# A causal mask added to the scores by VectorE in PSUM, and no longer by a TensorE product

## The chip, the cores and the metric

The kernel runs on one core of one Trainium2 chip. The metric is the device time of one execution in microseconds (us); a kernel's time is the median of several runs. The core's engines work side by side, each on its own queue of instructions, in the order written: TensorE (PE in the profile: PE for its matmuls, PEld for its weight loads), VectorE (DVE), ScalarE (ACT), GpSimd (POOL) and SyncE (SP), which issues DMAs. They wait for each other by semaphores. SBUF is the working memory; PSUM is the memory that TensorE writes its sums to, and VectorE and ScalarE can read and write it too.

## The reference, cut to what matters

The program is two blocks over a sequence of 1024 tokens with model width 1024. The second block has two kinds of attention, eight heads of each: softmax attention with a forgetting term ("fox"), and stick-breaking attention. Both are causal.

```python
# softmax ("fox"): keys up to and with the query's own position
logits = einsum('bhqd,bhkd->bhqk', q, k) * scale + F[..., :, None] - F[:, :, None, :]
logits = where(kpos[None, :] <= qpos[:, None], logits, -inf)
p = softmax(logits, axis=-1)

# stick-breaking: keys strictly before the query's position
mask = kpos[None, :] < qpos[:, None]
z = einsum('bhqd,bhkd->bhqk', q, k) * scale
log_beta = log_sigmoid(z)
log_one_minus = where(mask, log_sigmoid(-z), 0.0)
after = lax.cumsum(log_one_minus, axis=3, reverse=True) - log_one_minus
weights = where(mask, exp(log_beta + after), 0.0)
```

Queries are done in blocks of 128. A block needs the keys up to its own block, and only the last 128 x 128 block of its scores, the one on the diagonal, holds masked positions.

## The kernel before, in words

The change touches the attention stage of the second block, which in the trace runs from about 1230 to 1780 us. The stage has 8 rounds, taken in turn from the two kinds: rounds 0, 2, 4 and 6 are stick-breaking, 1, 3, 5 and 7 softmax. A round does two heads with 8 query tiles each, so 16 tiles; there are 128 tiles in all, numbered g. Tile tt of a head (0 to 7) has scores of 128 queries by w = (tt + 1) * 128 keys. The scores lie in a pair of PSUM banks, `Z[g % 2]`: one pair has the name S in the profile, the other G.

The stage is one software pipeline with a step s for each tile, written out by hand. Each engine walks over the same steps and does in each what is listed here, in this order.

- TensorE (PE): the scores of tile s + 2 (`scores`, lines 2079 and 2080: a product with the high part of the queries and one with the low part, for each 512 columns; line 2082: the mask). Then a piece of the projection of queries, keys and values for the next round (`piece`, line 2052). Then the product of the copied probabilities of tile s - 1 with the values (`values`, line 2110). Then the transposes of the probabilities of tile s (`turned`, line 2092). At two steps of a round also the transposes of the values (line 2120) and of the output (line 2131).
- ScalarE (ACT), stick-breaking: `not_taken` of tile s + 1 (line 2271, sigmoid of the negated scores), `probs_copied` of tile s - 1 (line 2265, out of PSUM), `taken` of tile s + 1 (line 2276, sigmoid). Between them, at given steps, it rounds queries, keys and weights to their high parts (`q_high` 2244 and 2245, `k_high` 2251, `w_high` 2236), turns out the output of the round before (2297) and sums its squares (2289).
- VectorE (DVE), stick-breaking: `chain` of tile s + 1. It is a scan over the negated sigmoids (line 2508, called "first") and a product with the sigmoids ("made", line 2511). In softmax rounds it is one custom instruction (line 2501). At given steps also `evac` (line 2471, which empties the projection's bank J to SBUF), `q_low` after tile 6 and `k_low` after tile 11 (lines 2479 and 2486, the low parts, two instructions each for the two heads), and `out_of` (2522 to 2526). The evacuation of a half of the projection comes ahead of the chain of its step.
- GpSimd (POOL): the low part of the next weights (line 1989, `w_lo`) as soon as ScalarE has made the high part, and in softmax rounds the mask (below).

Apart from the very first pieces, the projection is summed in one bank, J. So TensorE can begin a new half of it only after VectorE has evacuated the one before.

The mask is a constant of 128 x 128 bf16 values (`maskb`, one for each kind: 0 where a key is allowed, a large value elsewhere). In softmax rounds 1, 3 and 5 GpSimd adds it to the forget sums ahead of time (`mask_in_sums` is true, line 1980). In the four stick-breaking rounds and the last softmax round TensorE adds it: a product of the identity (`identb`) with the mask into the diagonal block of the scores, as the last product of the group. That is 5 rounds of 16 tiles, 80 products.

A wait such as `S.wait(act, "pe", "z", g)` holds the engine named first until the engine named second has done the step with that name and number. `do` marks such a step on VectorE and `me` is VectorE's wait for one of its own.

Of the kernel before, what the change touches and what calls it, by code (L numbers as in the profile page):

```python
# [9 lines left out]
ALU = mybir.AluOpType  # L10
# [4 lines left out]
P = 128  # L15
# [144 lines left out]
def program(nc, a, out, known):  # L160
# [27 lines left out]
    identb, maskb = bits[:, 0, :].bitcast(BF16), bits[:, 1:3, :].bitcast(BF16)  # L188
# [31 lines left out]
    S = Steps(known)  # L220
# [230 lines left out]
    with nc.Block() as block:  # L451
# [1272 lines left out]
        TILES, STEPS, SHIFT = 2 * TT, 2 * TT * 2 * HEADS, 2  # L1724
# [34 lines left out]
        Z = [S2, G[1]]  # L1759
# [5 lines left out]
        def tile_of(g):  # L1765

            return X[g // TILES % 2], g % TILES // TT, g % TT
# [11 lines left out]
        def mask_in_sums(g):  # L1779

            return tile_of(g)[0] == "f" and g // TILES < ROUNDS - 1

        def last_group(g):
            return GROUP_AT[g][-1][0] if g >= 0 else -1
# [4 lines left out]
        def stream(s):  # L1789

            q, n = divmod(s + SHIFT, TILES)
            return q + 1, n
# [36 lines left out]
        def own_rows(hh):  # L1829
            return slice(HD * hh, HD * hh + HD)  # L1830
# [176 lines left out]
        def _(pe):  # L2007
# [17 lines left out]
            for x, name in enumerate(("out sum", "out scaled sum")):  # L2025
                S.wait(pe, "dve", name, KT - 1)
                for t in range(TT):
                    mm = pe.matmul(G[1][:, x * TT + t:x * TT + t + 1], bs[:, x, t * P:(t + 1) * P], ones[:, 0:1], start=True, stop=True)
# [29 lines left out]
            def read(g):  # L2058

                S.wait(pe, *(("dve", "first", g) if tile_of(g)[0] == "f" else ("act", "taken", g)))  # L2060

            def scores(g):

                x, hh, tt = tile_of(g)
                r = g // TILES
                (Qh, Ql, Ks, _), z, w = SETS[r % 2], Z[g % 2], (tt + 1) * P
                if g < 2:
                    S.wait(pe, "act", ("rstd12 copied", "rstd1 copied")[g], 1)
                else:
                    read(g - 2)  # L2070
                if g > TILES and g % TILES == 5:
                    S.wait(pe, "act", "outT", 2 * (r - 1))
                if g % TILES == 0:
                    S.wait(pe, "act", "k high", r)
                    S.wait(pe, "dve", "k low", r)
                t = slice(tt * P, (tt + 1) * P)
                for b in range((w + NB - 1) // NB):
                    cols = slice(b * NB, min(w, (b + 1) * NB))
                    pe.matmul(z[:, cols], Qh[hh][:, t], Ks[hh][:, cols], start=True, stop=False)  # L2079
                    mm = pe.matmul(z[:, cols], Ql[hh][:, t], Ks[hh][:, cols], start=False, stop=mask_in_sums(g) or tt // 4 != b)  # L2080
                if not mask_in_sums(g):
                    mm = pe.matmul(z[:, tt * P:w], identb, maskb[:, "fs".index(x), :], start=False, stop=True)
                S.mark("pe", "z", mm, g)

            def turned(g):
# [123 lines left out]
        def _(act):  # L2209
# [56 lines left out]

            def not_taken(g):
                w = (g % TT + 1) * P
                S.wait(act, "pe", "z", g)
                S.wait(act, "dve", "first", g - 2 if g % TILES else g - 1)  # L2270
                S.mark("act", "not", act.activation(nots[g % 2][:, 0:w], Z[g % 2][:, 0:w], ACT.Sigmoid, scale=-1.0), g)

# [142 lines left out]
        def _(v):  # L2415
            def do(name, ins, turn=None):
                S.mark("dve", name, ins, turn)
                return name

            def me(name, turn=None):  # L2420
                S.wait(v, "dve", name, turn)
# [51 lines left out]
            def q_low(q):  # L2473
                Qh, Ql = SETS[q % 2][0:2]
                S.wait(v, "pe", "z", TILES * (q - 1) - 1)
                for hh in range(2):
                    S.wait(v, "act", f"q high {hh}", q)
                    own = own_rows(hh)
                    ins = v.tensor_tensor(Ql[hh][own, :], qt[own, :], Qh[hh][own, :].bitcast(F32), ALU.subtract)
                do("q low", ins, q)  # L2480

            def k_low(q):
                Ks = SETS[q % 2][2]
                S.wait(v, "act", "k high", q)
                for hh in range(2):
                    ins = v.tensor_tensor(Ks[hh][other_rows(hh), :], qt[own_rows(hh), :], Ks[hh][own_rows(hh), :].bitcast(F32), ALU.subtract)
                do("k low", ins, q)

            def chain(g):
                x, hh, tt = tile_of(g)  # L2490
                w = (tt + 1) * P
                p = pr[g % 2][:, 0:w]
                if x == "f":
                    r = g // TILES
                    if mask_in_sums(g):
                        S.wait(v, "pool", "masked", g)
                    elif tt == 0:
                        v.wait_ge(nf_landed[hh], 16 * (r // 2 + 1))
                    S.wait(v, "pe", "turned", last_group(g - 2))
                    S.wait(v, "pe", "z", g)  # L2500
                    do("first", v.tensor_tensor_reduce(out=p, in0=(masked_sums if mask_in_sums(g) else fsum[hh])[:, 0:w], in1=Z[g % 2][:, 0:w], scale=1.0, scalar=1e30,
                                                       op0=ALU.add, op1=ALU.min, accum_out=mn[:, g % 2, :]), g)
                else:
                    S.wait(v, "act", "not", g)
                    if g % TILES:
                        me("made", g - 1)
                    n_ = nots[g % 2]
                    do("first", v.tensor_tensor_scan(left[:, T - w:T][:, ::-1], n_[:, 0:w][:, ::-1], n_[:, 0:w], 1.0, ALU.mult, ALU.bypass), g)
                    S.wait(v, "act", "taken", g)
                    me("first", g)  # L2510
                    do("made", v.tensor_tensor(p, p, left[:, T - w + 1:T + 1], ALU.mult), g)

            def out_of(g4):
                x, hh, t0 = tile_of(4 * g4)
                r, n0 = 4 * g4 // TILES, 4 * g4 % TILES
                S.wait(v, "pe", "values", last_group(4 * g4 + 3))
                if g4 % 4 == 0 and r:
                    S.wait(v, "pe", "out turned", 2 * r - 1)
                    S.wait(v, "act", "square", TT * r - 1)
                dst, src = ON[:, t0:t0 + 4, own_rows(hh)], V[:, 0:4 * HD].rearrange("p (b d) -> p b d", d=HD)  # L2520
                if x == "f":
                    do("row sums", v.reciprocal(rs[:, n0:n0 + 4], rs[:, n0:n0 + 4]), g4)
                    me("row sums", g4)
                    do("out", v.tensor_tensor(dst, src, rs[:, n0:n0 + 4].unsqueeze(2).to_broadcast([P, 4, HD]), ALU.mult), g4)
                else:
                    do("out", v.tensor_copy(dst, src), g4)
# [8 lines left out]
            for s in range(-TILES - SHIFT, STEPS + 1):  # L2535
                q, n = stream(s)
                if n == 0 and 1 <= q <= ROUNDS:
                    evac(q - 1, 5)
                if q < ROUNDS and n in EVAC_AT[q % 2]:
                    evac(q, EVAC_AT[q % 2][n])  # L2540
                if s >= 5 and s % 4 == 1:
                    out_of((s - 5) // 4)
                if 0 <= s + 1 < STEPS:
                    chain(s + 1)
                if q < ROUNDS:
                    if n == 7:
                        q_low(q)
                    if n == 12:
                        k_low(q)
                if s == -TILES:  # L2550
                    S.wait(v, "act", "f ln")
                    do("forget logs", v.scalar_tensor_tensor(g8, g8, 0.0, l8, ALU.min, ALU.subtract))
                    me("forget logs")
                    do("forget sums", v.tensor_tensor_scan(F8, g8, g8, 0.0, ALU.add, ALU.bypass))
                if s == STEPS - TT:
                    v.wait_ge(x2_landed, 16 * KT)
                if s >= STEPS - TT and s % 2:
                    normed((s - STEPS + TT) // 2)
                if s == STEPS - 2:
                    S.wait(v, "act", "square", TT * (ROUNDS - 1) - 1)  # L2560
                    do("sb squares", v.tensor_reduce(ss[:, 0, :], ssp.rearrange("p (i x) t -> p x t i", x=2)[:, 0], AX.X, ALU.add))
                if s == STEPS - 1:
                    S.wait(v, "act", "sb root")
                    do("sb rstd", v.reciprocal(ss[:, 0, :], ss[:, 0, :]))
                    me("sb rstd")
                    diagonals("sb", bs[:, 0, :], ss[:, 0, :])
# [775 lines left out]
```

## Time and profile before

| | us |
|---|---|
| Median of 3 runs | 2575.83 |
| Lowest and highest | 2574.42, 2577.51 |
| The profiled execution, its own time | 2574.28 |
| Its span in the profile | 2572.5 |
| TensorE busy (matmuls) | 2506.5 |
| VectorE busy | 1509.0 |
| ScalarE busy | 1030.1 |
| GpSimd busy | 1058.9 |

The span runs from the first to the last instruction of the profile. Busy time counts a matmul from its start to its modelled end, and neighbouring matmuls overlap, so what a product costs is read from the starts of the products around it. Granted clock is the share of full speed that TensorE was given. In a timeline row the columns are start, duration, engine, line, operation, output and inputs with their shapes, and the count of instructions merged into the row (x2 means two, back to back). In square brackets stands how long the engine sat idle before it, and what ended that. The letter before the arrow is the tile that is written. Some names are shared by buffers that lie at one place: `forget_sums` in a row of line 2271 or 2508 is the second buffer of negated sigmoids, and G is the second pair of score banks, the bank J, or the bank that the values' product is summed in, by the line.

### The profile page before, as it was taken

The numbers are of one execution on the slowest core, as the hardware profiler recorded it, in microseconds if no ns is written. First come the engines' busy times: TensorE is split into PE (matmuls) and PEld (weight loads), VectorE is DVE, ScalarE is ACT, GpSimd is POOL, SyncE is SP. The second block draws the span as 40 slices with busy tenths as digits, with TensorE's granted clock in tenths as the row PEclk, the third lists the DMA queues.
The fourth block names the chain that finished last, engine by engine and source line by source line (L and its number), as shares of the span: only waits on it lengthen the run. The fifth ranks groups of instructions, "written<-read, shape, count | busy, mean of one in ns | idle before, by whom it ended". The sixth has DMA issues, their size and how long they took to land. (4 is left out here: it accounts for less than half of the span.)

```text
span 2572.5 us, 31716 instructions
## 1 busy us (share of the span) xinstructions
PE 2506.5 (97%) x12610; PEld 2089.5 (81%) x12610; DVE 1509.0 (59%) x1462; ACT 1030.1 (40%) x1528; POOL 1058.9 (41%) x617
## 2 busy tenths in 40 slices
PE   8999999999999999999999999999989999999999
PEld 4888788888888888887788888887867888888887
DVE  5864557665666753445645545464986667675324
ACT  3421043435344430024455655565344444443214
POOL 3765453333434335543111111213467777862320
PEclk9999999999999999999999999999989999999999
DMA  8222231211212144342111011013212222235311
GB/s 343 82 89 72 95 96 52 68 58 66 71 68 76 50 181 146 98 139 82 34 42 42 34 41 42 25 51 131 103 45 92 81 74 99 74 109 228 129 41 66
DMA packets 66238, 226.07 MB, mean 88 GB/s; under 512 B 7816, under 2 KB 11784, under 8 KB 64816
## 3 DMA queue, kind: packets, MB, share of 16 engines
q1 hardware_dynamic: 49824, 169.00, 18.5%
q10 hardware_dynamic: 16272, 55.09, 6.0%
q8 instruction: 99, 1.62, 0.3%
q14 instruction: 43, 0.35, 0.0%
HBM read 174.22 MB, written 45.65 MB: 85 GB/s over the span
## 5 line engine op out<-in xcount | busy, mean ns | idle before, releaser
L264 POOL TENSOR_TENSOR w_hi<-w_raw,ones 128x1024 fp32r<-128x1024 f32 x67 | 178.7, 2667 | 525.8 <-PE G L238 471.9
L269 POOL TENSOR_TENSOR w_lo<-w_raw,w_hi 128x1024 fp32r<-128x1024 f32 x88 | 239.2, 2718 | 198.0 <-ACT w_hi L263 192.8
L238 PE MATMUL G<-H_hi,w_hi 128*128 128x512 f32 x928 | 290.1, 394 | 1.0 <-ACT silu_zB L724 0.7
L238 PE MATMUL G<-H_lo,w_hi 128*128 128x512 f32 x928 | 285.9, 389 | 0.0
L238 PE MATMUL G<-H_hi,w_lo 128*128 128x512 f32 x928 | 285.8, 389 | 0.0
L238 PEld LDWEIGHTS G<-H_lo,w_hi 128*128 128x128 f32 x928 | 174.2, 188 | 36.6
L238 PEld LDWEIGHTS G<-H_hi,w_lo 128*128 128x128 f32 x928 | 174.2, 188 | 36.5
L238 PEld LDWEIGHTS G<-H_hi,w_hi 128*128 128x128 f32 x928 | 171.6, 188 | 36.9 <-issue 3.7
L1989 POOL TENSOR_TENSOR w_lo<-w_raw,w_hi 128x1024 fp32r<-128x1024 f32 x24 | 60.1, 2506 | 319.8 <-ACT w_hi L2236 319.8
L2110 PEld LDWEIGHTS G<-att_v,probsT 128*128 128x128 f32 x1152 | 147.0, 192 | 24.5 <-ACT probsT L2265 13.8
L2052 PE MATMUL G<-A_hi,w_hi 128*128 128x512 f32 x368 | 152.8, 415 | 9.4 <-DVE projected L2471 8.4
L2110 PE MATMUL G<-att_v,probsT 128*128 128x64 f32 x1152 | 145.7, 272 | 12.2 <-ACT probsT L2265 9.6
L2052 PE MATMUL G<-A_hi,w_lo 128*128 128x512 f32 x368 | 144.9, 394 | 0.0
L2052 PE MATMUL G<-A_lo,w_hi 128*128 128x512 f32 x368 | 144.5, 393 | 0.0
L2265 ACT ACTIVATE probsT<-U 128x512 f32<-128x512 f32 (+1 forms) x192 | 86.7, 486 | 128.3 <-PE U L2092 127.7
L2851 PE MATMUL G<-sums_hi,up_hi_S 128*128 128x512 f32 x260 | 102.4, 394 | 5.3 <-POOL up_lo_S L2801 4.8
L2851 PE MATMUL G<-sums_lo,up_hi_S 128*128 128x512 f32 x260 | 102.1, 393 | 0.0
L2851 PE MATMUL G<-sums_hi,up_lo_S 128*128 128x512 f32 x260 | 102.1, 393 | 0.0
L2801 POOL TENSOR_TENSOR up_lo<-up_raw,up_hi 128x512 fp32r<-128x512 f32 x66 | 88.3, 1339 | 17.7 <-ACT up_hi L1909 17.7
L1274 ACT ACTIVATE exps<-exps 128x1024 f32<-128x1024 f32 x60 | 61.9, 1057 | 71.2 <-DVE exps L1433 64.3
L2052 PEld LDWEIGHTS G<-A_hi,w_hi 128*128 128x128 f32 x368 | 70.2, 191 | 22.4 <-DVE projected L2471 7.0
L2092 PE MATMUL U<-ident,probs 128*128 128x128 f32 x576 | 85.6, 276 | 0.0
(594 smaller groups left out, 6263.4 us busy)
## 6 DMA issues: line engine op xcount, KB each, us to landing
w_raw<-w_in SPq DMA_DIRECT2D x65, 512.0 KB, 3.3
up_raw<-w_up SPq DMA_DIRECT2D x44, 512.0 KB, 5.0
pre_raw<-w_in SPq DMA_DIRECT2D x30, 512.0 KB, 3.3
act_d<-made SPq DMA_DIRECT2D x22, 512.0 KB, 2.9
wm<-w_mod SPq DMA_DIRECT2D x8, 1024.0 KB, 18.5
w_raw<-w_out SPq DMA_DIRECT2D x16, 512.0 KB, 3.3
x_d<-x ACTq DMA_DIRECT2D x16, 512.0 KB, 2.9
x<-x_d SPq DMA_DIRECT2D x16, 512.0 KB, 9.1
```

Of the source, the lines that this page charges most:

```text
L238: mm = nc.tensor.matmul(dst[:, n * NB:n * NB + c], w[:, k, :], m[:, k, n * NB:n * NB + c], start=first, stop=last)
L264: eng.tensor_tensor(dst, src, ones.unsqueeze(1).to_broadcast([P, kt, P]), ALU.mult)
L269: nc.gpsimd.tensor_tensor(w_lo[:, slot, 0:kt, :], w_raw[:, slot, 0:kt, :], w_hi[:, slot, 0:kt, :].bitcast(F32), ALU.subtract).then_inc(w_r ...
L1274: S.mark("act", f"exps {w} {e}", act.activation(E[e], src, ACT.Exp, scale=1.0 / GATE_NORM), h)
L1989: g.tensor_tensor(w_lo[:, j % 2], w_raw[:, j % 2], w_hi[:, j % 2].bitcast(F32), ALU.subtract).then_inc(w_ready, 1)
L2052: mm = pe.matmul(bank, w[:, j % 2, k, :], m[:, k, cols], start=first, stop=last)
L2092: mm = pe.transpose(bank[:, b * P:(b + 1) * P], pr[g % 2][:, (b0 + b) * P:(b0 + b + 1) * P], ident)
L2110: mm = pe.matmul(V[:, at:at + HD], pT[c % 2][:, b, :], v[:, b0 + b, own_rows(hh)], start=b0 + b == 0, stop=b0 + b == tt)
L2265: S.mark("act", "p copied", act.activation(pT[c % 2][:, 0:n, :], blocks_of(bank_of_u(("p", c)), n), ACT.Copy), c)
L2801: S.mark("pool", f"low {name}", g_.tensor_tensor(slot_lo[name], slab_source(p, name), slot_hi[name].bitcast(F32), ALU.subtract), p)
L2851: mm = pe.matmul(dst, w[name][:, j, :], up_moving(name, x, j), start=first and j == 0 and w is slot_hi and x == 0, stop=j == PAIRS_OF - 1 ...
```

## The change

The identity product goes. The last low-part product of each 512 columns now closes its group, and the scores are signalled right after it. VectorE gets a new step `z_masked(g)`: it waits for the scores of tile g and adds the mask to their diagonal block, in place in PSUM. It is called for tile g + 1 right behind the first instruction of tile g's chain, so in a stick-breaking round between the scan and the product of tile g. ScalarE's `not_taken` waits for that step and no longer for TensorE. In the last softmax round the custom instruction waits for it. Rounds 1, 3 and 5 keep the mask in the forget sums. For tile 0 the step is called ahead of the first chain.

```diff
                     pe.matmul(z[:, cols], Qh[hh][:, t], Ks[hh][:, cols], start=True, stop=False)
-                    mm = pe.matmul(z[:, cols], Ql[hh][:, t], Ks[hh][:, cols], start=False, stop=mask_in_sums(g) or tt // 4 != b)
-                if not mask_in_sums(g):
-                    mm = pe.matmul(z[:, tt * P:w], identb, maskb[:, "fs".index(x), :], start=False, stop=True)
+                    mm = pe.matmul(z[:, cols], Ql[hh][:, t], Ks[hh][:, cols], start=False, stop=True)
                 S.mark("pe", "z", mm, g)
...
             def not_taken(g):
                 w = (g % TT + 1) * P
-                S.wait(act, "pe", "z", g)
+                S.wait(act, "dve", "z masked", g)
                 S.wait(act, "dve", "first", g - 2 if g % TILES else g - 1)
...
+            def z_masked(g):
+
+                if g == STEPS or mask_in_sums(g):
+                    return
+                x, _, tt = tile_of(g)
+                block = Z[g % 2][:, tt * P:(tt + 1) * P]
+                S.wait(v, "pe", "z", g)
+                do("z masked", v.tensor_tensor(block, block, maskb[:, "fs".index(x), :], ALU.add), g)
...
                     S.wait(v, "pe", "turned", last_group(g - 2))
-                    S.wait(v, "pe", "z", g)
+                    if mask_in_sums(g):
+                        S.wait(v, "pe", "z", g)
+                    else:
+                        me("z masked", g)
                     do("first", v.tensor_tensor_reduce(...), g)
+                    z_masked(g + 1)
                 else:
                     ...
                     do("first", v.tensor_tensor_scan(left[:, T - w:T][:, ::-1], n_[:, 0:w][:, ::-1], n_[:, 0:w], 1.0, ALU.mult, ALU.bypass), g)
+                    z_masked(g + 1)
                     S.wait(v, "act", "taken", g)
                     me("first", g)
                     do("made", v.tensor_tensor(p, p, left[:, T - w + 1:T + 1], ALU.mult), g)
...
+                if s + 2 == 0:
+                    z_masked(0)
                 if 0 <= s + 1 < STEPS:
                     chain(s + 1)
```

## Rows read from the trace of the kernel before

**Rows 1.** The page, busy time of each engine, its share of the span, instructions.

```profile
PE 2506.5 (97%) x12610; PEld 2089.5 (81%) x12610; DVE 1509.0 (59%) x1462; ACT 1030.1 (40%) x1528; POOL 1058.9 (41%) x617
```

**Rows 2.** Busy time by stretches: round 4, last round; then PEclk, DMA share, GB/s.

```profile
1514.00:1584.00 70.00, 67.50 (x423) 57.90 (x422) 48.13 (x47) 42.82 (x87) 7.99 (x4) 1.00 0.11 38
1724.00:1772.00 48.00, 41.62 (x304) 37.15 (x302) 20.37 (x44) 32.09 (x80) 21.14 (x9) 0.93 0.55 209
```

**Rows 3.** Line 2082, one bank pair; timelines of TensorE, with the mask and without.

```profile
L2082 PE MATMUL S<-bf_constants x40: 229/230/303, 1230.5 to 1766.9; 128*128 128x128 bf16 x40
...
1568.64 0.28 PE L2080 MATMUL G<-k_parts,q_lo 128*128 128x256 f32 x1
...
1569.11 0.39 PE L2052 MATMUL G<-A_lo,w_hi 128*128 128x512 f32 x1
...
1302.71 0.28 PE L2080 MATMUL G<-k_parts,q_lo 128*128 128x256 f32 x1
...
1303.07 0.40 PE L2052 MATMUL G<-A_lo,w_hi 128*128 128x512 f32 x1
```

**Rows 4.** Waits from 1200 to 1790: who for whom, us, times, longest.

```profile
PE G L2052 <- DVE projected L2471: 8.4, 11, 2.8
```

**Rows 5.** Timeline of round 4, TensorE's wait for the copied probabilities of tile 2.

```profile
1535.17 0.88 PE L2110 MATMUL G<-att_v,probsT 128*128 128x64 f32 x6 [1.23 <-ACT probsT L2265]
```

**Rows 6.** Timeline of round 4, tiles 6 and 7, all engines.

```profile
1542.18 2.03 DVE L2508 TENSOR_TENSOR_SCAN left_over<-not_taken 128x896 f32<-128x896 f32 x1 [0.66 <-ACT not_taken L2271]
...
1544.19 0.39 PE L2080 MATMUL G<-k_parts,q_lo 128*128 128x512 f32 x1
1544.31 1.09 DVE L2511 TENSOR_TENSOR probs<-probs,left_over 128x896 f32<-128x896 f32 x1
...
1545.32 2.44 DVE L2479 TENSOR_TENSOR q_lo<-projected,q_hi 64x1024 fp32r<-64x1024 f32 x2
...
1546.90 3.10 POOL L1989 TENSOR_TENSOR w_lo<-w_raw,w_hi 128x1024 fp32r<-128x1024 f32 x1 [25.05 <-ACT w_hi L2236]
...
1547.85 0.69 DVE L2471 SCALAR_TENSOR_TENSOR projected<-G,rstd 128x512 f32<-128x512 f32 x1
...
1548.60 0.50 PE L2052 MATMUL G<-A_hi,w_hi 128*128 128x512 f32 x1 [0.55 <-DVE projected L2471]
```

**Rows 7.** Timeline of round 4, product of tile 11 and the low keys.

```profile
1566.24 0.69 DVE L2511 TENSOR_TENSOR probs<-probs,left_over 128x512 f32<-128x512 f32 x1
...
1566.81 2.38 POOL L1989 TENSOR_TENSOR w_lo<-w_raw,w_hi 128x1024 fp32r<-128x1024 f32 x1 [16.81 <-ACT w_hi L2236]
1566.97 4.54 DVE L2486 TENSOR_TENSOR k_parts<-projected,k_parts 64x1024 fp32r<-64x1024 f32 x2
```

**Rows 8.** Timeline of round 4, tiles 11 to 13.

```profile
1569.23 0.82 ACT L2271 ACTIVATE forget_sums<-G 128x768 f32<-128x768 f32 x1
...
1571.53 0.60 ACT L2265 ACTIVATE probsT<-U 128x512 f32<-128x512 f32 x1 [1.48 <-PE U L2092]
...
1571.60 0.69 DVE L2471 SCALAR_TENSOR_TENSOR projected<-G,rstd 128x512 f32<-128x512 f32 x1
...
1572.21 1.48 DVE L2508 TENSOR_TENSOR_SCAN left_over<-not_taken 128x640 f32<-128x640 f32 x1
...
1574.54 1.00 PE L2110 MATMUL G<-att_v,probsT 128*128 128x64 f32 x8
```

**Rows 9.** Groups by line and shape: count, busy us, mean ns, idle before.

```profile
L2511 DVE TENSOR_TENSOR probs<-probs,left_over 128x128 f32<-128x128 f32 x8 | 2.3, 292 | 2.7 <-ACT probs L2276 1.8 <-ACT forget_sums L2271 0.5
```

**Rows 10.** Timeline of round 0, tiles 6 and 7.

```profile
1260.46 1.09 DVE L2511 TENSOR_TENSOR probs<-probs,left_over 128x896 f32<-128x896 f32 x1
...
1260.99 0.39 PE L2080 MATMUL G<-k_parts,q_lo 128*128 128x512 f32 x1
...
1263.24 2.93 POOL L1989 TENSOR_TENSOR w_lo<-w_raw,w_hi 128x1024 fp32r<-128x1024 f32 x1 [22.07 <-ACT w_hi L2236]
...
1264.75 0.50 PE L2052 MATMUL G<-A_hi,w_hi 128*128 128x512 f32 x1
```

## The prediction

> **What bounds the kernel now.** I read the page first, then the busy time by stretches over the attention stage, then the line of the removed product, then the waits, and last the timeline of one stick-breaking round, instruction by instruction. TensorE is busy for 97% of the span [rows 1]. In a stick-breaking round of 70 us it is busy for 67.5 us at a granted clock of 1.00, while VectorE is busy for 48.1 us and ScalarE for 42.8 us [rows 2]. So the end is set by TensorE's stream, and a product taken from it is worth something. But the 2.5 us that TensorE does not work in such a round are a few waits at fixed places: for the probabilities that ScalarE copies back (1.23 us at 1535.17), and for VectorE to empty the one bank J in which the next round's projection is summed (0.55 us at 1548.60) [rows 5, 6]. Over the stage TensorE waits 8.4 us, 11 times, for that evacuation [rows 4]. At these places VectorE is the later one, and the change gives VectorE more to do there.
>
> I number the 16 tiles of a round 0 to 15 (widths 128 to 1024, twice). In step s TensorE does scores(s+2), a piece of projection, values(s-1), turned(s). VectorE does the scan and the product of tile s+1. ScalarE does, strictly in this order, `not` of s+1, the copy of the turned probabilities of s-1, `taken` of s+1.
>
> **What is removed.** 80 products of the identity with the mask [rows 3]; the row shows the 40 of one pair of banks, and the other pair has as many. What one costs TensorE is not its 0.23 us, since products overlap. From the start of the last low product of a 256-wide tile to the start of the second projection product behind it, it is 1569.11 - 1568.64 = 0.47 us with the mask and 1303.07 - 1302.71 = 0.36 us without [rows 3]. So 0.11 us each, 8.8 us for 80 if all were kept.
>
> Not all are kept. A saving ahead of a wait whose releaser is not TensorE itself only makes the wait longer. Going through round 4 (1514 to 1584): tiles 0 to 4 lie ahead of the turning of the previous round's output, which starts the chain of ScalarE that ends in the wait of 1535.17, so they are kept. Tiles 5 and 6 are lost in that wait and in the one for the evacuation behind it, 7 and 8 in the wait of 1548.60. Tiles 9 and 10 are kept. Tiles 11 to 14 are lost, since the evacuation at 1571.60 to 1572.29 [rows 8] releases the piece behind the scores of tile 14. Tile 15 is kept. That is 8 kept masks in rounds 2, 4 and 6 and 7 in round 0, where tile 0 stands before a wait: 31 x 0.11 = 3.4 us. In the last round (softmax, no projection) TensorE is busy for 41.6 of 48 us [rows 2], so its waits are long enough to swallow the savings. VectorE's next instruction there waits for a transpose that TensorE does after the scores anyway, so the additions hide. I put both at nothing; the bounds are 16 x 0.11 = 1.8 us gained and 16 x 0.29 = 4.6 us lost.
>
> **What is added.** 80 additions on VectorE of 128 columns. The nearest row is the 128-wide tensor_tensor of the same engine, 0.292 us [rows 9]. The bounds are nothing (it would fill the gap that the scan-to-product dependency leaves anyway, 1544.21 to 1544.31 in [rows 6]) and 0.69 us, the 512-wide evacuation out of PSUM. I take 0.29. If its scores are ready when the scan ends, the addition fills that gap, its start overlapping the scan's end by 0.09 us as neighbouring instructions of this engine do, and the product behind it is hardly moved. 14 of the 16 additions of a round are of this kind or stand where VectorE waits for ScalarE anyway, and cost nothing. Two places do not.
>
> **Place one, tile 7, the projection's bank.** The added instruction stands between scan 6 and product 6 and waits for the scores of tile 7. Behind it on VectorE stand product 6, the two halves of `q_low`, and the evacuation of J for which TensorE already waits. Scan 6 ends at 1544.21. The last low product of tile 7 ends at 1544.19 + 0.39 = 1544.58, so the addition runs from 1544.62 to 1544.91, and product 6 starts at 1544.82, not 1544.31: half a microsecond late [rows 6]. The first half of `q_low` then runs from 1545.83 to 1547.05, not 1545.32 to 1546.54.
>
> Now GpSimd comes in. Its split of the weights (`w_lo`) starts at 1546.90, released by ScalarE, which this delay does not touch. Before, it met the second half of `q_low` already running: it took 3.10 us, not 2.38 [rows 6, 7], and VectorE was not held. After, it is waiting when the first half ends, with the second not begun. What happens then is in the same trace: at 1566.81 GpSimd started 0.12 us before a VectorE product ended, and the `k_low` that came next took 4.54 us for two halves that need 2.44 as `q_low` does: it stood still for 2.10 us, until about the end of GpSimd's instruction at 1569.19 [rows 6, 7]. So the second half of `q_low` ends where GpSimd has had its turn, 1547.05 + 2.1 + 1.22 = 1550.37. The evacuation follows to 1551.15, and TensorE's piece goes at 1551.20, not 1548.60: 2.60 us lost. The addition itself has one input in PSUM, as the evacuation has, which ran its plain 0.69 us inside GpSimd's instruction.
>
> The Trainium skill ("SBUF — State Buffer", section "Who interferes with whom") says it as a rule: a VectorE instruction with two SBUF inputs and a GpSimd instruction that reads SBUF exclude each other, and the one that issues first holds the port for its whole length. These rows agree. By that rule alone the order at 1547 decides; did they share the port by halves, the place would cost about the 0.5 us of delay.
>
> In round 0 the same place has no wait yet, but the step is shorter: the scores of tile 7 end at 1260.99 + 0.39 = 1261.38, when product 6 had already been running since 1260.46. The first half of `q_low` would run 1262.63 to 1263.85, with GpSimd waiting from 1263.24 (0.6 us, no close call), the second half ends at 1267.17, the evacuation at 1267.95, and the piece of 1264.75 goes at 1268.01: 3.26 us [rows 10]. Sum of place one: 3.3 + 3 x 2.6 = 11.1 us.
>
> **Place two, tile 13, the copied probabilities.** Before, `not` 13 needed the scores alone and ran at 1569.23. Now it needs addition 13, which stands behind scan 12, and scan 12 stands behind `k_low` and an evacuation: 1572.21 to 1573.69. Addition 13 ends at 1573.89, `not` 13 takes 1573.93 to 1574.75. Behind it on ScalarE stands the copy of the turned probabilities of tile 11, which was done at 1572.13: it now takes 1574.65 to 1575.25. TensorE wanted them at 1574.54 and gets them at 1575.28 [rows 8]. 0.74 us, in each of the four rounds: 3.0 us. An addition of no length would still cost 0.45 us here.
>
> **The sum.** 11.1 + 3.0 - 3.4 = +10.7 us. The profiled execution took 2574.28 us (span 2572.5 and 1.8 around it), which gives 2585.0. It stands 1.5 us under the median of the three runs, 2575.83, so I say 2586 for a median.
>
> **Rivals.**
> *The port falls the other way (20%).* In rounds 2, 4 and 6 GpSimd is ahead of the second half of `q_low` by only 0.15 us; with an addition under 0.14 us, or scores signalled earlier, it comes too late. Against it: 0.12 us were enough at 1566.93 [rows 7]. Then place one costs 0.5 us in three rounds and 3.3 in round 0: 3.3 + 1.5 + 3.0 - 3.4 = +4.4, near 2580.
>
> *Only the gain (15%).* VectorE is idle for 22 of 70 us [rows 2] and the additions are done in these; the two places do not reach TensorE, because it comes early to them. That decides if product 6 starts no later than now and `not` 13 is not behind `k_low`. Against it: both are fixed by the order on the engines. It gives -3.4 us with the kept masks and -8.8 with all: 2572 to 2567. This is the rival on the other side.
>
> *Costs and gain even out (13%).* Place two only, with place one absorbed, is 3.0 - 3.4 = -0.4: 2575.5.
>
> *The forecast (52%)*: 2586, its own range 2583 to 2590. The upper end has an addition of 0.69 us: 0.4 us more at each of eight places, +3.2.
>
> A difference under 0.2% (5.2 us, 2570.7 to 2581.0) can't be told from none. Faster: most of the second rival, 0.14. Within: the evened case and over half of the first rival, 0.25. Slower: the forecast and the rest of the first, 0.61. The range 2571 to 2591 leaves out most of the second rival and a little above.
>
> **What would show it.** In the trace after: product 6 of an even round starts 0.5 us after scan 6 ends; the second half of `q_low` is long (x2 about 4.5 us, not 2.44); TensorE's wait for J in step 6 is near 3 us in four rounds, and TensorE's total wait for the evacuation goes from 8.4 to about 19 us; the values of tile 11 wait 0.7 us or more for the copy; GpSimd's split there takes 2.4 to 2.6 us. The softmax rounds 1, 3 and 5 keep their length. The forecast is wrong if `q_low` keeps 2.44 us, if the addition takes well under 0.2 us, or if the stick-breaking rounds are not longer than their 70 us.

## The result, and the profile after

The changed kernel takes 2594.19 us (median of 4 runs, 2593.89 to 2596.45), the kernel before on the same chip 2576.67 us (4 runs, 2574.42 to 2580.73). The ratio is 1.0064, 95% interval 1.0051 to 1.0077: about 16.5 us slower (the two medians lie 17.5 us apart). The forecast was 2586 with a range of 2571 to 2591. The direction was right; the time lies above the range.

The profiled execution of the changed kernel has a span of 2592.6 us where the one of before has 2572.5. The page's first part answers to [rows 1]. TensorE has 80 instructions less, VectorE 80 more and 17 us more of work, and TensorE's busy time has not fallen, although products were removed:

```profile
PE 2507.3 (97%) x12530; PEld 2093.3 (81%) x12530; DVE 1526.1 (59%) x1542; ACT 1030.9 (40%) x1528; POOL 1055.7 (41%) x617
```

The added instruction, by form, over the attention stage (operation and shape, count, busy us, mean ns, idle before it). It answers to [rows 9], from which it was priced at 292 ns:

```profile
L2494 DVE TENSOR_TENSOR G<-G,bf_constants 128x128 f32<-128x128 f32 x40 | 11.5, 288 | 16.2 <-PE G L2080 15.8
L2494 DVE TENSOR_TENSOR S<-S,bf_constants 128x128 f32<-128x128 f32 x40 | 11.4, 285 | 16.5 <-PE S L2080 16.1
```

The waits from 1200 to 1810 (who for whom, us, times, longest) answer to [rows 4]. TensorE's wait for the evacuated bank went from 8.4 to 22.1 us, forecast about 19. Its wait for the copied probabilities, 9.6 us in 12 waits before, is 3.2 us more in 17:

```profile
PE G L2052 <- DVE projected L2469: 22.1, 16, 3.7
PE G L2108 <- ACT probsT L2263: 12.8, 17, 2.1
```

**Place one** in the timeline of round 4 (start us, us, what, idle before) answers to [rows 6]. Round 4 began later, so only distances compare:

```profile
1552.05 2.02 DVE L2519 TENSOR_TENSOR_SCAN left_over<-not_taken 128x896 f32<-128x896 f32 x1 [0.61 <-ACT not_taken L2269]
...
1554.56 0.30 DVE L2494 TENSOR_TENSOR G<-G,bf_constants 128x128 f32<-128x128 f32 x1 [0.49 <-PE G L2080]
...
1554.77 1.08 DVE L2523 TENSOR_TENSOR probs<-probs,left_over 128x896 f32<-128x896 f32 x1
...
1555.77 4.51 DVE L2477 TENSOR_TENSOR q_lo<-projected,q_hi 64x1024 fp32r<-64x1024 f32 x2
...
1556.77 2.42 POOL L1989 TENSOR_TENSOR w_lo<-w_raw,w_hi 128x1024 fp32r<-128x1024 f32 x1 [24.67 <-ACT w_hi L2234]
...
1560.37 0.69 DVE L2469 SCALAR_TENSOR_TENSOR projected<-G,rstd 128x512 f32<-128x512 f32 x1
...
1561.12 0.80 PE L2052 MATMUL G<-A_hi,w_hi 128*128 128x512 f32 x1 [3.33 <-DVE projected L2469]
...
1561.71 0.63 PE L2052 MATMUL G<-A_lo,w_hi 128*128 128x512 f32 x1
```

Scan 6 ends at 1554.07; the addition waits for TensorE's scores and the product follows 0.70 us after the scan. GpSimd's split, pending before the second half of `q_low` can begin, goes first, and the two halves of `q_low` take 4.51 us for 2.44. All of this was forecast. The last two rows were not, though one of [rows 3] shows what belongs there: the products behind the wait take 0.63 us and start 0.43 apart, where others take 0.39 and start 0.23 apart.

One thing at this place was not read before the change: GpSimd's turn cost VectorE time there as well, only later. Scan 7, right behind the evacuation, took 3.69 us in the kernel before, where GpSimd's split lasts until 1550.00 [rows 6], and 2.28 us in the changed one, in which GpSimd has finished by then. The first row is of before, the second of after:

```profile
1548.46 3.69 DVE L2508 TENSOR_TENSOR_SCAN left_over<-forget_sums 128x1024 f32<-128x1024 f32 x1
1560.98 2.28 DVE L2519 TENSOR_TENSOR_SCAN left_over<-forget_sums 128x1024 f32<-128x1024 f32 x1
```

So VectorE stood still for 1.4 us behind the evacuation before, and stands still for 2.1 us ahead of it now. What the change moved is the place of the stop, from where TensorE does not wait to where it does.

**Place two** in the same round, which answers to [rows 8]:

```profile
1586.74 1.48 DVE L2519 TENSOR_TENSOR_SCAN left_over<-not_taken 128x640 f32<-128x640 f32 x1
...
1588.14 0.28 DVE L2494 TENSOR_TENSOR G<-G,bf_constants 128x128 f32<-128x128 f32 x1
...
1588.45 0.81 ACT L2269 ACTIVATE forget_sums<-G 128x768 f32<-128x768 f32 x1 [4.82 <-DVE G L2494]
...
1589.15 0.59 ACT L2263 ACTIVATE probsT<-U 128x512 f32<-128x512 f32 x1
...
1589.80 1.10 PE L2108 MATMUL G<-att_v,probsT 128*128 128x64 f32 x8 [0.57 <-ACT probsT L2263]
```

**The clock.** Two stretches of 4 us, behind the long wait of round 4 and of round 0. The columns are those of [rows 2]; the seventh is the granted clock. TensorE is busy for nearly all of each, and at 1.2 GHz (0.50) all through the first. In rounds 2 and 6 the clock behind the wait is 0.62 (it falls a little later there) and 0.50:

```profile
1561.00:1565.00 4.00, 3.88 (x9) 3.11 (x10) 3.90 (x5) 0.28 (x1) 0.00 (x0) 0.50 0.16 61
1269.00:1273.00 4.00, 3.85 (x11) 3.12 (x11) 3.90 (x5) 0.28 (x1) 0.00 (x0) 0.57 0.10 40
```

**Where the span went.** I measure a round from one turning of its values to the next. Stick-breaking rounds 0, 2, 4 and 6 went from 68.8, 72.1, 72.1 and 69.3 us to 75.3, 76.4, 77.1 and 74.3: +6.5, +4.3, +5.0 and +5.0. The three softmax rounds between them lost 1.1 us together (0.24, 0.27 and 0.62), and the last round 0.7. That sums to the 18.9 us by which the stage ends later (1777.43 to 1796.30); the other 1.2 us of span lie behind the stage and were not followed. The scores of tiles 0 and 1 of a round are made ahead of its turning, so they count to the round ahead: in the kernel before, the mask products of these tiles of round 4 stand at 1509.95 and 1514.46, its turning at 1516.66.

### The profile page after: what moved, and what is told of

It is laid out like the page before. It is cut to its first block and busy times, and to the rows that moved or that the text cites. A ratio compares the mean times of both kernels' runs of the same rounds, so it can differ in the third digit from the quotient of the medians.

```text
span 2592.6 us, 31636 instructions
## 1 busy us (share of the span) xinstructions
PE 2507.3 (97%) x12530; PEld 2093.3 (81%) x12530; DVE 1526.1 (59%) x1542; ACT 1030.9 (40%) x1528; POOL 1055.7 (41%) x617
## 5 line engine op out<-in xcount | busy, mean ns | idle before, releaser
L2052 PE MATMUL G<-A_hi,w_hi 128*128 128x512 f32 x368 | 151.6, 412 | 22.4 <-DVE projected L2469 22.1
```

The source lines that it names most:

```text
L2052: mm = pe.matmul(bank, w[:, j % 2, k, :], m[:, k, cols], start=first, stop=last)
```

## The experiments

Each kernel was timed side by side with the kernel before on the same chip, 5 to 11 executions each (medians of before 2578.6 for e1 to e4, 2577.6 for e5 to e8). An interval of a ratio is some 0.09 to 0.14% on either side, 2.3 to 3.6 us, so the ratios tell the large steps apart, and the smaller ones are read from the lengths of rounds in the profiles, one execution for each kernel. The order here is that of the argument.

**e1: the gain by itself.** The kernel before without the 80 products and with nothing in their place.

```
-  mm = pe.matmul(z[:, cols], Ql[hh][:, t], Ks[hh][:, cols], start=False, stop=mask_in_sums(g) or tt // 4 != b)
-  if not mask_in_sums(g):
-      mm = pe.matmul(z[:, tt * P:w], identb, maskb[:, "fs".index(x), :], start=False, stop=True)
+  mm = pe.matmul(z[:, cols], Ql[hh][:, t], Ks[hh][:, cols], start=False, stop=True)
```

> The kernel before with the 80 mask products left out and nothing in their place, so the mask of the stick-breaking rounds and of the last softmax round is not applied. It gives the gain alone. My step of the prediction (31 masks kept at 0.11 us): 3.4 us faster, near 2573. Rival, every mask is kept: 8.8 us faster, near 2568. Rival, all is absorbed by waits: no difference.

Measured: 2574.63 us, ratio 0.9983 (0.9974 to 0.9992), so 4.4 us. The stage took 3.4 us less from its first turning to its end than before. So the waits swallow about half of the 8.8 us or more, as forecast; both rivals, 8.8 and nothing, lie outside the interval. By rounds it is less tidy: rounds 2, 4 and 6 lost 0.8 us each, the softmax rounds 0.2 to 0.3 each, the last round 0.9, and round 0 grew by 0.5.

**e2: place one by itself.** The kernel before, with its products, and the addition of tile 7 alone, four in all. The mask is added there a second time.

```
+  if g % TILES == 6:
+      z_masked(g + 1)          # between scan 6 and product 6
   S.wait(v, "act", "taken", g)
...
-  S.wait(act, "pe", "z", g)    # in not_taken
+  S.wait(act, *(("dve", "z masked", g) if g % TILES == 7 else ("pe", "z", g)))
```

> The kernel before, product kept, with one VectorE addition in each stick-breaking round: that of tile 7, between scan and product of tile 6 (it adds the mask a second time). 4 additions of 80. If place one (the wait for the scores of tile 7, then GpSimd taking the port ahead of the second half of q_low, then a clock at half) is nearly all of the loss: +18 to +21 us, near 2596, with waits of 2.8 to 3.7 us for the bank and a granted clock of 0.5 for some 5 us behind each. Rival, the loss comes from 80 additions spread over the stage: under +2 us.

Measured: 2595.86 us (2594.61 to 2597.52), ratio 1.0068 (1.0054 to 1.0081). Four additions of the 80 cost as much as the whole change, products kept. Its timeline in round 4 has the same chain:

```profile
1556.98 4.52 DVE L2479 TENSOR_TENSOR q_lo<-projected,q_hi 64x1024 fp32r<-64x1024 f32 x2
...
1557.96 2.46 POOL L1989 TENSOR_TENSOR w_lo<-w_raw,w_hi 128x1024 fp32r<-128x1024 f32 x1 [25.04 <-ACT w_hi L2236]
...
1562.33 0.50 PE L2052 MATMUL G<-A_hi,w_hi 128*128 128x512 f32 x1 [3.19 <-DVE projected L2471]
...
1564.63 0.63 PE L2052 MATMUL G<-A_hi,w_lo 128*128 128x512 f32 x1
```

The wait is 3.19 us, and here too the products behind it grow to 0.63 us, after some at 0.39.

**e3: the port.** The changed kernel, all 80 additions, but GpSimd's split starts only once the low queries are done.

```
   S.wait(g, "act", "w high", j)
+  if n == 7 and q % 2:
+      S.wait(g, "dve", "q low", q)
```

> The changed kernel, and in the stick-breaking rounds GpSimd's split of the weights at this place waits until q_low is done. The addition of tile 7 stays where it is. If the port is the cause: q_low takes 2.44 us again, TensorE waits 1.1 us at the bank and not 3.3, no stretch at half clock there, and the time is near 2579. Rival, the wait of VectorE for the scores alone costs the time: it stays near 2594.

Measured: 2579.48 us, ratio 1.0007 (0.9998 to 1.0016). The addition is as late as in the changed kernel, and yet `q_low` has its plain length, the wait is 1.27 us, and the product behind it is a fast one (second fence: the 4 us behind it):

```profile
1549.31 2.45 DVE L2479 TENSOR_TENSOR q_lo<-projected,q_hi 64x1024 fp32r<-64x1024 f32 x2
...
1551.90 2.37 POOL L1991 TENSOR_TENSOR w_lo<-w_raw,w_hi 128x1024 fp32r<-128x1024 f32 x1 [26.26 <-DVE q_lo L2479]
...
1552.59 0.50 PE L2054 MATMUL G<-A_hi,w_hi 128*128 128x512 f32 x1 [1.27 <-DVE projected L2471]
```

```profile
1552.50:1556.50 4.00, 3.91 (x26) 3.54 (x27) 4.00 (x3) 0.33 (x1) 1.77 (x1) 1.00 0.29 95
```

So it is GpSimd's turn inside `q_low` that costs most, not the addition: what is left of its delay is 0.5 to 0.6 us a round (e3 against e5 below). The Trainium skill ("SBUF — State Buffer", section "Who interferes with whom") has the two exclude each other for whole instructions; the traces here agree (4.51 to 4.56 us with GpSimd pending between the halves, 2.45 without).

**e4: the clock, with narrow products.** The changed kernel, which in the long wait of place one does 96 more products of 128 columns on scores that are then done again.

```
-  for b in range((w + NB - 1) // NB):
+  for b in (0,) * 13 if x == "s" and g % TILES == 8 else range((w + NB - 1) // NB):
```

> The changed kernel with the two score products of tile 8 in each stick-breaking round done 13 times over, 24 more 128-wide products (about 2.8 us of TensorE) in the stretch in which it sits idle for the bank. The bank comes no earlier. If the idle time is what takes the clock down, the projection products behind it start 0.23 us apart again and not 0.43, and the kernel with 96 more products is 8 to 9 us faster than the changed one, near 2586. Rival, the clock falls for another reason: the same as the changed kernel or slower, 2594 to 2597.

Measured: 2592.18 us (2589.23 to 2594.43), ratio 1.0053 (1.0039 to 1.0067). Less came back than expected, and the 0.11% against the changed kernel lies within the intervals; the profiled execution is the fastest of the five (2589.23). In it rounds 2, 4 and 6 became shorter by 1.6, 2.3 and 2.3 us, but round 0 only by 0.1: behind its wait the clock was low all the same. Round 0 and round 4:

```profile
1269.00:1273.00 4.00, 3.51 (x9) 2.80 (x10) 3.96 (x4) 0.28 (x1) 0.00 (x0) 0.57 0.22 87
1559.50:1563.50 4.00, 3.72 (x24) 3.33 (x25) 3.90 (x5) 0.28 (x1) 0.00 (x0) 1.00 0.22 87
```

**e8: the clock, with wide products.** The same with 12 products of 512 columns ahead of the scores of tile 8.

```
+  if x == "s" and g % TILES == 8:
+      for _ in range(12):
+          pe.matmul(z[:, 0:NB], Qh[hh][:, t], Ks[hh][:, 0:NB], start=True, stop=True)
```

> The changed kernel with 12 products of 512 columns (0.23 us each, 2.8 us) ahead of the scores of tile 8 in each stick-breaking round, in the place of 24 narrow ones. The narrow ones kept the clock in rounds 2, 4 and 6 and not in round 0 (1.05 us idle left). If it is the idle time that counts, wide ones give the same: clock lost in round 0 alone. If narrow products count for less than wide ones, round 0 keeps its clock too, some 2 us less: near 2588.

Measured: 2587.28 us (2585.74 to 2590.51), ratio 1.0042 (1.0028 to 1.0056). Now the clock holds in round 0 as well, and the kernel with 48 more wide products is 0.22% faster than the changed one (about 0.19% on either side for that difference):

```profile
1269.00:1273.00 4.00, 4.00 (x29) 3.65 (x28) 3.52 (x4) 0.51 (x2) 0.00 (x0) 1.00 0.00 1
```

Nothing in VectorE's chain differs: the bank comes free as late as in the changed kernel. By the rounds of the two profiles, what the filler gives back is the clock alone: 2.7, 1.5, 2.3 and 2.3 us in the four rounds, 8.8 in all. This one is near the forecast of 2586, which had no clock in it.

**e5: addition 7 moved.** In the changed kernel it now stands at the start of step 7, behind `q_low` and the evacuation.

```
                 else:
+                    if g % TILES == 7:
+                        z_masked(g)
                     S.wait(v, "act", "not", g)
                     ...
-                    z_masked(g + 1)
+                    if g % TILES not in (6,):
+                        z_masked(g + 1)
```

> The changed kernel with one call moved: the addition of tile 7 of a stick-breaking round stands behind q_low and the evacuation, ahead of scan 7, and no longer between scan 6 and product 6. All 80 additions are still there. If place one (port and clock) is the loss: waits at the bank under 0.8 us, no half clock, and only place two stays, 4 x 0.57 us, against a gain of 3.4: 1 us under the kernel before, ratio 0.9996. Rival, 79 other additions cost something too: over 1.002.

Measured: 2576.82 us, ratio 0.9996 (0.9987 to 1.0005). Moving four additions by a few instructions takes back the whole loss. TensorE still waits for the copied probabilities 18 times (13.3 us): place two is untouched.

**e6: additions 7 and 13 moved.** The latter goes ahead of scan 12.

```
+                    if g % TILES == 12:
+                        z_masked(g + 1)
                     S.wait(v, "act", "not", g)
...
+                    if g % TILES not in (6, 12):
```

> As the kernel with tile 7 moved, and the addition of tile 13 stands ahead of scan 12, no longer behind it. Place two goes: TensorE no longer waits for the copied probabilities of tile 11 (0.57 us, 4 times). The additions are then free, and the time is that of the kernel without any mask: 3.4 us under before, ratio 0.9983 to 0.9990. Rival, additions ahead of a scan only move the wait: no better than 0.9996.

Measured: 2573.69 us, ratio 0.9986 (0.9977 to 0.9995): faster than before by 3.6 us. The step from e5 is within the intervals of the two; in the profiles rounds 2, 4 and 6 are 0.9 us shorter each. The order at place one is the one of before again, GpSimd's split beside a plain `q_low`; at place two the copied probabilities are there when TensorE wants them, with no wait in the last row:

```profile
1543.25 2.45 DVE L2477 TENSOR_TENSOR q_lo<-projected,q_hi 64x1024 fp32r<-64x1024 f32 x2
...
1544.84 3.10 POOL L1989 TENSOR_TENSOR w_lo<-w_raw,w_hi 128x1024 fp32r<-128x1024 f32 x1 [24.67 <-ACT w_hi L2234]
...
1546.54 0.50 PE L2052 MATMUL G<-A_hi,w_hi 128*128 128x512 f32 x1 [0.75 <-DVE projected L2469]
...
1569.87 0.29 DVE L2494 TENSOR_TENSOR G<-G,bf_constants 128x128 f32<-128x128 f32 x1
...
1570.19 0.82 ACT L2269 ACTIVATE forget_sums<-G 128x768 f32<-128x768 f32 x1 [3.39 <-DVE G L2494]
...
1572.19 1.00 PE L2108 MATMUL G<-att_v,probsT 128*128 128x64 f32 x8
```

**e7: both moved, and one more split held.** A wait of 2.8 us at the start of round 0 was in the kernel before already [rows 4]. Here GpSimd's split of that place waits for scan 1.

```
+  if n == 1 and q == 1:
+      S.wait(g, "dve", "first", 1)
```

> Both additions moved, and in round 0 GpSimd's first split of the weights waits for the scan of tile 1, which stands still behind it in every version (TensorE waits 2.8 us for the bank there, then runs about 4 us at half clock). If port and clock work there as at place one: the wait falls to about 0.8 us, the clock stays full, 2 + 2 us less: ratio 0.997. Rival, the later split is waited for by TensorE instead: no gain over both moved.

Measured: 2570.76 us (2567.63 to 2572.30), ratio 0.9973 (0.9961 to 0.9984): the fastest of all, 7.0 us under before and 23 under the changed kernel. Against e6 it gains 0.13%, which the intervals do not tell from none; in the profiles round 0 is 1.9 us shorter than in e6, by the wait, 0.85 us for 2.83. What the clock adds there is not shown, since e6 had kept its clock behind that wait in its profile:

```profile
1242.75 0.69 DVE L2525 TENSOR_TENSOR_SCAN left_over<-forget_sums 128x256 f32<-128x256 f32 x1 [4.35 <-ACT forget_sums L2271]
...
1243.58 2.63 POOL L1991 TENSOR_TENSOR w_lo<-w_raw,w_hi 128x1024 fp32r<-128x1024 f32 x1 [14.17 <-DVE left_over L2525]
...
1244.62 0.50 PE L2054 MATMUL G<-A_hi,w_hi 128*128 128x512 f32 x1 [0.85 <-DVE projected L2471]
```

## Why the prediction was wrong

**The step that failed is the sum**: "11.1 + 3.0 - 3.4 = +10.7 us". Its terms were right in kind and nearly in size. It had a missing term: its 11.1 us for place one priced a longer wait of TensorE at the wait's own length, with every product behind it at full speed. The runs showed that the products behind such a wait run at half clock, and that this costs 1.5 to 2.7 us a wait: 8.8 us for four by the rounds of the profiles, 5.7 us by the ratios. Rounds 2, 4 and 6 show this best, since round 0 also has a clock that differs between executions (below). Each line is a difference of round lengths between two kernels, and together they are the whole way from before to after:

```
term                           from two kernels   rounds 2, 4, 6, us   sum    forecast
gain less what hides it        e6 - before        -0.8  -0.8  -0.8     -2.4   -2.0
place two                      e5 - e6             0.9   0.9   0.9      2.7    2.2
place one, full clock          e8 - e5             2.6   2.7   2.6      7.9    7.8
clock behind the long wait     after - e8          1.5   2.3   2.3      6.1    none
all                            after - before      4.3   5.0   5.0     14.2    8.0
```

The forecast of the gain is 6 kept products a round here, since those of tiles 0 and 1 count to the round ahead.

The measured times say the same with wider bounds. From the ratios in the same order: -3.6, 2.6, 11.9 and 5.7 us, in all 16.5, where the forecast had -3.4, 3.0, 11.1 and nothing. (The last two join ratios taken on different occasions, and a difference of two such ratios is uncertain by 3 to 5 us.) The three terms that the forecast had come to 10.9 us against its 10.7, closer than these bounds can claim; the fourth is what it lacked.

Point by point:

- *What is removed*: right in kind, 3.4 us in the stage against 3.4, but that the totals agree is partly luck. In e1 rounds 2, 4 and 6 gave 0.8 us each and the softmax rounds ahead 0.2 to 0.3 (two products at 0.11, those of tiles 0 and 1), 3.0 together against 2.6 forecast. The last round gave 0.9, put at nothing. Round 0 grew by 0.5 where 0.8 less was forecast: behind its wait of 2.84 us the clock was 0.50 and then 0.77 in two stretches of 4 us, in the kernel before 0.57 and then 1.00.
- *What is added*: right; 285 to 288 ns for 292. It fills the gap between scan and product, as said: at 1588.14 it begins 0.08 us before the scan ends.
- *Place one*: right in each link. Product 6 is 0.70 us behind the scan's end instead of 0.10 (forecast half a microsecond late), `q_low` takes 4.51 us, GpSimd 2.42, and the waits are 3.33 us three times and 3.71 in round 0. That the port is the cause is shown by e3, that this place carries the loss by e2 and e5. The rival in which the port falls the other way asked for a plain `q_low` in three rounds, which no round of the changed kernel shows. e3 has it in all four, round 0 too, and is 1.8 us above before; the rival's own terms give 4 x 0.5 + 3.0 - 3.4 = 1.6 us for that. "VectorE was not held" holds for `q_low` alone: scan 7 behind it was (3.69 us for 2.28). It changes no term, as TensorE does not wait for it there.
- *Place two*: right; 0.85 to 0.91 us a round between e5 and e6, against 0.74.
- *Only the gain*, and *even out*: refuted for this kernel. Both describe what e6 (-3.6 us) and e5 (-1.0 us) do, once the additions stand elsewhere.
- *The range*: its upper end held 3.2 us for a longer addition, and nothing for the clock. The trace of before had the row that would have priced it. [Rows 4] name a longest wait of 2.8 us, and behind it, in round 0:

```profile
1242.90 0.79 PE L2052 MATMUL G<-A_hi,w_hi 128*128 128x512 f32 x1 [2.75 <-DVE projected L2471]
...
1243.49 0.63 PE L2052 MATMUL G<-A_lo,w_hi 128*128 128x512 f32 x1
```

```profile
1242.00:1246.00 4.00, 3.10 (x7) 2.48 (x8) 3.49 (x5) 0.40 (x1) 0.00 (x0) 0.60 0.43 131
```

I had this wait in hand and did not read the products behind it. The waits that I forecast for place one, 0.55 + 2.60 = 3.15 us in three rounds, were longer than this one. With 0.20 us lost on each of the products and the slow values behind, as in the timeline of round 4 after, about 2 us a round (an estimate) would have been added, which gives a forecast near 2594.

The Trainium skill ("TensorE: Matmul & The Clock Gate", section "HAM oscillation — how this bites in real kernels") tells of a kernel in which a wait for a DMA ahead of each group of products brings the clock down every single time. The traces agree for the four long waits of the changed kernel, 3.33 to 3.71 us, with 0.50 to 0.62 in the 4 us behind them, and against them 1.00 behind the 1.27 us of e3. They do not agree on every time: behind one and the same wait of 2.83 us the clock fell in some profiles and held in one (below).

## What to carry to other kernels

Price a wait of TensorE twice: by its length, and by the speed of the products behind it, which is read off behind the longest wait of the same kind in the trace of before. When an instruction is put into an engine's stream, follow what stands behind it up to the next point at which another engine competes for the same port: half a microsecond of delay moved GpSimd's turn, and VectorE's stop of 2.1 us with it, ahead of what TensorE waits for. And before such a change is dropped, move the few additions that hurt: four of 80 carried the loss, and moving eight turned +0.64% into -0.14%.

## What the hardware showed unexpectedly

The clock behind a wait is not the same in every execution. The wait at the start of round 0 is 2.83 or 2.84 us in the profiles of the changed kernel, e1, e3, e4, e5, e6 and e8. Behind it the first product takes 0.79 to 0.80 us in five of them, with a clock of 0.50 to 0.60 in the next 4 us. In e3 it takes 0.50, and the clock falls a little later (0.69). In e6 it takes 0.50 too, and the clock stays at 1.00. The changed kernel and e6:

```profile
1242.89 0.80 PE L2052 MATMUL G<-A_hi,w_hi 128*128 128x512 f32 x1 [2.83 <-DVE projected L2469]
```

```profile
1244.69 0.50 PE L2052 MATMUL G<-A_hi,w_hi 128*128 128x512 f32 x1 [2.83 <-DVE projected L2469]
```

That may be a part of why the profiled span of the changed kernel grew by 20.1 us and the measured time by 16.5; another is that the profiled execution of before (2574.28) is a fast one of its kernel. Neither was tested, and one profile of each kernel can't settle it. Nor is it settled why the narrow filler of e4, with 1.05 us of idle time left in round 0, lost the clock there, and the wide one of e8, with 1.01 us left, did not: width, the place of the filler and chance remain.
